# Attention scores as three rounded passes, with the next pair's projections ahead of the last mix

## The chip, the cores and the metric

The kernel runs on one core of one Trainium2 chip. The metric is the device time of one execution in microseconds (us); lower is better. Times below are of one profiled execution where a trace is read, and the median of three runs for the kernel as a whole.

## The reference

Two layers of a mixer and an MLP, on 512 latent tokens and 256 context tokens of width 1024. In each layer a projection of the normalised input is split among three mixers (latent attention, a Fourier mix, a state space), whose outputs are gated, summed and projected; then an MLP with squared ReLU. The change concerns the attention alone:

```python
qn, qr = mla_q(za, lp["q_norm"], lp["w_uq"])      # 8 heads, 64 + 32 rotary
qr = apply_rope(qr, cos[:, None, :], sin[:, None, :])
kn, v, kr = mla_kv(za, lp["kv_norm"], lp["w_ukv"]) # one rotary key for all heads
kr = apply_rope(kr, cos, sin)
...
s = jnp.einsum('bqhd,bkhd->bhqk', q_nope, k_nope) + jnp.einsum('bqhr,bkr->bhqk', q_rope, k_rope)
p = jax.nn.softmax(s * ATTN_SCALE, axis=-1)
return jnp.einsum('bhqk,bkhd->bqhd', p, v)
```

Latent queries attend to context and latent keys (768), context queries to context keys alone (256). In layer 1 only latent queries are wanted (n is 512 there, 768 in layer 0).

## The kernel before, in words

All engines run programs written out by hand, and wait for each other by semaphores; the order on each engine is the order of the code. Each large product multiplies a weight tile of 128 output channels by up to 768 tokens. To keep float32 accuracy, a product is made in three passes of rounded parts (type fp32r): high weights by high tokens, high weights by low tokens, low weights by high tokens (`product`, line 464, and `project`, line 918). The high part is a copy to fp32r, by ScalarE, the low part is a subtraction, value less high part, by VectorE. GpSimd splits the weights (lines 1284, 1287) from tiles that SyncE loads into a ring; a tile's place comes free when `w_used` is marked.

The tail of the projections (`slots`): after the gates, `("key", 0)`, `("query", 0)`, `("query", 1)` project the keys and both queries of the first pair of heads, and the last gate tile (23) follows. A slot's bank of PSUM is `TURN[s % 4]`.

Attention runs over four pairs of heads (`h2`). One pair has units (head j, block b of 128 queries): 12 in layer 0, of which the last four have 256 keys, and 8 in layer 1. For a unit u, TensorE makes the scores (line 1048, plain float32, 96 partitions, in banks 0 and 1), VectorE the row maximum (`maximum`, line 2034), ScalarE the exponent (line 1661), VectorE the reciprocal and the division (line 2050), TensorE the transposes (line 1096, bank 2), ScalarE their copy (line 1684), and TensorE the mix with the values (`mix`, line 1063, bank 3), in thirds for each group of four units. TensorE's order is scores(u + 2), perhaps a third of a mix, then the transposes of u. In layer 0 the modulation's products (`pe_ada`, line 582) lie between.

At the hand-over from one pair to the next, TensorE projects the first query of the next pair (`project_q(h2 + 1, 0)`, bank 0) among the last units, then does the modulation's turn (line 592, layer 0 only) and the last mix; then the keys (`project_k`, bank 2), the second query (bank 1), scores(0), the projection of the values (`project_v`, line 944, bank 3), scores(1). Of the queries, ScalarE copies the 64 plain rows (line 1591) and VectorE rotates the 32 rotary rows (`rotate`, lines 1824, 1826, 1829), straight from PSUM; ScalarE copies the keys (lines 1583, 1584). The output of a pair in bank 3 is rounded by ScalarE (`oah`, line 1698), and its low part is VectorE's (`oal`, line 2064, `ol_ready`); the next values may be written to the bank after that.

In pair 1 ScalarE also rounds the outputs of the state space and the Fourier mix (`osh`, `ofh`, line 1676), one a unit, and in pair 2 VectorE makes their low parts (`osl`, `ofl`, line 2057). The branches (`branch`) need these.

## Time and profile before

| | |
|---|---|
| median of three runs | 2192.99 us (2192.02 to 2195.16) |
| the profiled execution | 2193.51 us, its span 2191.7 us |
| TensorE busy | 98% of the span, 12388 products |
| VectorE, ScalarE, GpSimd busy | 56%, 23%, 41% |
| granted TensorE clock, mean | 0.996 |
| line 464 (all large products), share of the chain that ended last | 67% |
| line 1048 (scores), share of that chain | 3% |

The busy time of an engine is the union of its instructions. The chain is followed back from the last instruction, at each step to what released it; the time on it is time that the end depended on. The attention of layer 0 stands at 420 to 594 us, that of layer 1 at 1594 to 1721 us.

### The profile page before, as it was taken

The numbers are of one execution on the slowest core, as the hardware profiler recorded it, in microseconds if no ns is written. First come the engines' busy times: TensorE is split into PE (matmuls) and PEld (weight loads), VectorE is DVE, ScalarE is ACT, GpSimd is POOL, SyncE is SP. The second block draws the span as 40 slices with busy tenths as digits, with TensorE's granted clock in tenths as the row PEclk, the third lists the DMA queues.
The fourth block names the chain that finished last, engine by engine and source line by source line (L and its number), as shares of the span: only waits on it lengthen the run. The fifth ranks groups of instructions, "written<-read, shape, count | busy, mean of one in ns | idle before, by whom it ended". The sixth has DMA issues, their size and how long they took to land.

```text
span 2191.7 us, 30382 instructions
## 1 busy us (share of the span) xinstructions
PE 2147.6 (98%) x12388; PEld 1759.2 (80%) x12388; DVE 1225.6 (56%) x1887; ACT 505.0 (23%) x814; POOL 898.6 (41%) x492
## 2 busy tenths in 40 slices
PE   6999999999999999999999999999999999999998
PEld 4888888766688888888888888888766787888886
DVE  7998981455563445364565424594255757253353
ACT  3115021354400220110201102322355212010010
POOL 2441442200144344443444443545411356766662
PEclk9999999999999999999999999999999999999998
DMA  7363354233453422122223254546310552322221
GB/s 279 103 136 99 123 191 138 92 109 117 166 197 118 172 105 95 67 75 90 77 87 101 73 220 184 116 141 207 125 39 14 195 187 81 114 96 96 96 97 67
DMA packets 105390, 267.79 MB, mean 122 GB/s; under 512 B 22650, under 2 KB 42490, under 8 KB 103470
## 3 DMA queue, kind: packets, MB, share of 16 engines
q1 hardware_dynamic: 68928, 190.87, 25.4%
q10 hardware_dynamic: 36334, 75.07, 10.5%
q8 instruction: 98, 1.61, 0.3%
q14 instruction: 30, 0.25, 0.0%
HBM read 227.56 MB, written 37.88 MB: 121 GB/s over the span
## 4 chain that ended last, share of the span: by engine, by line
PE 90%; DVE 7%; DMA 1%; SPq 1%; ACT 1%; issue 0%; POOL 0%; DVEq 0%; ACTq 0%; POOLq 0%
PE ps L464 67%; PE ps L1048 3%; PE ps L918 3%; PE ps L1063 2%; PE ps L1096 2%; PE ps L582 2%; PE ps L473 2%; DVE t_out L2170 1%; DVE t_in L2170 1%; PE ps L479 1%; PE ps L956 1%; PE ps L777 1%; PE ps L991 1%; PE ps L944 1%; PE ps L907 1%; DMA ada_first<-in_ada_w 1%
## 5 line engine op out<-in xcount | busy, mean ns | idle before, releaser
L1284 POOL TENSOR_SCALAR whi<-raw 128x1024 fp32r<-128x1024 f32 x244 | 272.3, 1116 | 1240.3 <-PE ps L464 679.0
L1287 POOL TENSOR_TENSOR wlo<-raw,whi 128x1024 fp32r<-128x1024 f32 x244 | 626.8, 2569 | 20.4
L464 PE MATMUL ps<-hh,whi 128*128 128x512 f32 (+1 forms) x1560 | 465.3, 355 | 0.3 <-DVE ada L608 0.3
L464 PE MATMUL ps<-hh,wlo 128*128 128x512 f32 (+1 forms) x1560 | 462.8, 353 | 0.0
L464 PE MATMUL ps<-hl,whi 128*128 128x512 f32 (+1 forms) x1560 | 461.7, 352 | 0.0
L464 PEld LDWEIGHTS ps<-hh,whi 128*128 128x128 f32 x1560 | 254.8, 188 | 44.1 <-ACT mr L1718 1.0
L464 PEld LDWEIGHTS ps<-hl,whi 128*128 128x128 f32 x1560 | 254.3, 188 | 42.8 <-issue 0.2
L464 PEld LDWEIGHTS ps<-hh,wlo 128*128 128x128 f32 x1560 | 254.2, 188 | 42.1
L2103 DVE SCALAR_TENSOR_TENSOR x<-ps,ada,x 128x512 f32<-128x512 f32 x120 | 75.5, 659 | 343.0 <-PE ps L464 342.9
L464 PE MATMUL ps<-midh,whi 128*128 128x512 f32 (+1 forms) x768 | 233.8, 358 | 1.8 <-DVE midl L2133 1.8
L464 PE MATMUL ps<-midh,wlo 128*128 128x512 f32 (+1 forms) x768 | 231.2, 355 | 0.0
L464 PE MATMUL ps<-midl,whi 128*128 128x512 f32 (+1 forms) x768 | 230.9, 355 | 0.0
L2129 DVE TENSOR_TENSOR ms<-mr 128x768 f32<-128x768 f32 (+1 forms) x64 | 76.2, 1190 | 182.6 <-ACT mr L1718 182.5
L2133 DVE TENSOR_TENSOR midl<-ms,midh 128x768 fp32r<-128x768 f32 (+1 forms) x64 | 172.7, 2699 | 2.2
L1718 ACT ACTIVATE mr<-ps 128x768 f32<-128x768 f32 (+1 forms) x64 | 45.1, 705 | 520.2 <-PE ps L464 510.7
L464 PEld LDWEIGHTS ps<-midh,whi 128*128 128x128 f32 x768 | 126.3, 188 | 25.3 <-DVE midl L2133 3.0
L464 PEld LDWEIGHTS ps<-midl,whi 128*128 128x128 f32 x768 | 126.5, 188 | 22.0
L464 PEld LDWEIGHTS ps<-midh,wlo 128*128 128x128 f32 x768 | 125.8, 188 | 21.7
L1048 PE MATMUL ps<-kk,qq 96*128 96x512 f32 (+1 forms) x288 | 104.7, 483 | 1.2 <-ACT pr L1661 1.2
L1492 ACT ACTIVATE gt<-ps,b_gate 128x768 f32<-128x768 f32 (+1 forms) x48 | 38.2, 797 | 271.2 <-PE ps L464 259.7
L2034 DVE TENSOR_REDUCE mx<-ps 128x1 f32<-128x768 f32 (+1 forms) x80 | 68.0, 850 | 54.7 <-PE ps L1048 54.2
L1048 PEld LDWEIGHTS ps<-kk,qq 96*128 96x128 f32 x288 | 48.6, 189 | 40.4 <-issue 35.9
(251 smaller groups left out, 2833.5 us busy)
## 6 DMA issues: line engine op xcount, KB each, us to landing
raw<-in_w_main SPq DMA_DIRECT2D x244, 512.0 KB, 3.3
ada_gap<-in_ada_w SPq DMA_DIRECT2D x40, 512.0 KB, 10.0
ada_mixer<-in_ada_w SPq DMA_DIRECT2D x32, 512.0 KB, 4.0
g_d<-gt ACTq DMA_DIRECT2D x24, 384.0 KB, 2.4
gl<-g_d ACTq DMA_DIRECT2D x8, 1152.0 KB, 5.9
ada_first<-in_ada_w SPq DMA_DIRECT2D x16, 512.0 KB, 15.4
cout_d<-cz SPq DMA_DIRECT2D x12, 512.0 KB, 5.1
cout<-cout_d ACTq DMA_DIRECT2D x6, 1024.0 KB, 9.1
```

The source lines that it names most:

```text
L464: ins = pe.matmul(ps[:, p % 4, a:b], ww[:, w % W_SLOTS, kw * P:(kw + 1) * P], xx[:, kx, a:b], start=(first and i == 0 and j == 0), stop=(l ...
L473: pe.matmul(ps[:, p, a:b], ww[:, w % W_SLOTS, k * P:(k + 1) * P], hh[:, k, a:b], start=(k == 0 and ww is whi), stop=False)
L582: ins = pe.matmul(sums[32 * j:32 * j + 32], svec[:, u, :], w[:, 256 * j:256 * j + 256], start=(u == 0), stop=(u == 7))
L918: ins = pe.matmul(ps[:, p, a:b], ww, xx[:, a:b], start=(first and i == 0), stop=(last and i == 2))
L1048: ins = pe.matmul(ps[:, u % 2, a:e], qq[0:96, j, b * P:b * P + P], kk[0:96, j, a:e], start=True, stop=True)
L1284: pool.tensor_scalar(whi[:, u, :], raw[:, u % 2, :], 1.0, 0.0, ALU.mult, ALU.add).then_inc(w_split.sem, 1)
L1287: pool.tensor_tensor(wlo[:, u, :], raw[:, u % 2, :], whi[:, u, :].bitcast(F32), ALU.subtract).then_inc(w_split.sem, 1)
L1718: act.activation(mr[:, m % 2, 0:n], pair(t % mlp_pairs(l), n), ACT.Relu).then_inc(relu_ready.sem, relu_ready.mark((l, q, m)))
L2034: dve.tensor_reduce(mx[:, c:c + 1], ps[:, u % 2, (0 if b < 4 else 512):TOK], AXX, ALU.max).then_inc(max_ready.sem, max_ready.mark((l, h2, u)))
L2103: ins = dve.scalar_tensor_tensor(x[:, m, a:b], pair(p, n)[:, a:b], ada[:, l, ada_tile(row, m), s:s + 1], x[:, m, a:b], ALU.mult, ALU.add)
L2129: dve.tensor_tensor(ms[:, m % 2, 0:n], mr[:, m % 2, 0:n], mr[:, m % 2, 0:n], ALU.mult).then_inc(msq_ready.sem, msq_ready.mark((l, q, m)))
L2133: dve.tensor_tensor(midl[:, m, 0:n], ms[:, m % 2, 0:n], midh[:, m, 0:n].bitcast(F32), ALU.subtract).then_inc(midl_ready.sem, midl_ready.ma ...
```

## The change

1. Scores are made in three passes of rounded parts: high query by high key, low query by high key, high query by low key, all into the same bank. For this ScalarE rounds each query whole (96 rows, after the rotation) and the keys of each head (64 rows), and VectorE subtracts to get the low parts of both. The rotation's result goes back to PSUM. The rotary rows of the keys are split once a layer by VectorE, after the copies of y.
2. At a hand-over the second query and the keys are projected before the turn and the last mix. VectorE's queue there has both rotations, then low query 0, low keys 0, low query 1, low keys 1, all ahead of the modulation's sum and `oal`; ScalarE's has the four high parts ahead of `oah`.
3. The last gate tile goes ahead of the first pair's keys and queries. After them TensorE projects the values of pair 0 into the bank that lies free, and only then makes scores(0) and scores(1). ScalarE copies the values ahead of the first exponent.
4. The low parts of the Fourier outputs move from pair 2 to the end of pair 3; the first branch product waits for those of the state space alone, the second for these.

The diff, without signals' declarations and repeated forms:

```diff
+VALUES_PAIR = (2, 3)
...
     return (gates[:before - 1] + [("y", i) for i in range(3)] + gates[before - 1:before - 1 + between]
-            + [("glu", o) for o in range(3)] + gates[before - 1 + between:-1]
-            + [("key", 0), ("query", 0), ("query", 1), gates[-1]])
+            + [("glu", o) for o in range(3)] + gates[before - 1 + between:]
+            + [("key", 0), ("query", 0), ("query", 1)])
...
+        kkh = rest("kkh", 15360, [P, 2, TOK], F32R)
+        kkl = (rest("kkl0", 86016, [P, TOK], F32R), at("kkl1", HREG + 27648, [P, TOK], F32R))
+        qqh = rest("qqh", 49152, [P, 2, TOK], F32R)
+        qql = [at(f"qql{j}", HREG + 30720 + 3072 * j, [P, TOK], F32R) for j in range(2)]
+        qqt = [at(f"qqt{j}", HREG + 30720 + 3072 * j, [P, TOK]) for j in range(2)]
...
-                    if j:
+                    if j and h2 == 0:
...
-                ins.then_inc(k_done.sem, k_done.mark((l, h2)))
-
-            def project_v(h2):
+                if h2:
+                    ins.then_inc(w_used.sem, w_used.mark(t0 + pair_tile(h2)))
+                else:
+                    ins.then_inc(k_done.sem, k_done.mark((l, h2)))
...
+                    pe.wait_ge(os_lo.sem, os_lo.at((l, 2)))
+                elif seq == 1:
                     pe.wait_ge(os_lo.sem, os_lo.at((l, 5)))
...
-                if h2:
-                    project_k(h2)
-                    project_q(h2, 1)
-                pe.wait_ge(ropes.sem, ropes.at(("q", l, h2, 0, 2)))
-                pe.wait_ge(q_act.sem, q_act.at((l, h2, 0)))
-                pe.wait_ge(k_act.sem, k_act.at((l, h2)))
-                if h2 == 0:
-                    pe.wait_ge(ropes.sem, ropes.at(("k", l, 3)))
...
-                    if u == 1:
-                        pe.wait_ge(ropes.sem, ropes.at(("q", l, h2, 1, 2)))
-                        pe.wait_ge(q_act.sem, q_act.at((l, h2, 1)))
+                    if u < 2:
+                        pe.wait_ge(q_lo.sem, q_lo.at((l, h2, j)))
+                        pe.wait_ge(k_lo.sem, k_lo.at((l, h2, j)))
                     if u >= 2:
                         pe.wait_ge(exp_ready.sem, exp_ready.at((l, h2, u - 2)))
                     keys = spans(TOK) if b < 4 else [(512, 768)]
-                    for a, e in keys:
-                        ins = pe.matmul(ps[:, u % 2, a:e], qq[0:96, j, b * P:b * P + P], kk[0:96, j, a:e],
-                                        start=True, stop=True)
+                    qh, ql = (v[0:96, b * P:b * P + P] for v in (qqh[:, j], qql[j]))
+                    for i, (q, k) in enumerate(((qh, kkh[:, j]), (ql, kkh[:, j]), (qh, kkl[j]))):
+                        for a, e in keys:
+                            ins = pe.matmul(ps[:, u % 2, a:e], q, k[0:96, a:e], start=(i == 0), stop=(i == 2))
                     ins.then_inc(sc_done.sem, sc_done.mark((l, h2, u)))
...
-                scores(0)
-                if h2:
+                if h2 == 0:
+                    pe.wait_ge(g_ready.sem, g_ready.at((l, N_GATES - 1)))
+                    if l:
+                        pe.wait_ge(k_lo.sem, k_lo.at((l, 0, 1)))
+                    project_v(0, VALUES_PAIR[l])
+                    pe.wait_ge(kr_split.sem, kr_split.at((l, "low")))
+                    pe.wait_ge(k_lo.sem, k_lo.at((l, 0, 1)))
+                    scores(0)
+                    scores(1)
+                else:
+                    scores(0)
                     pe.wait_ge(ol_ready.sem, ol_ready.at((l, h2 - 1)))
-                elif l == 0:
-                    pe.wait_ge(ropes.sem, ropes.at(("q", 0, 0, 1, 2)))
-                    pe.wait_ge(q_act.sem, q_act.at((0, 0, 1)))
-                project_v(h2)
-                if l == 0 and h2 == 0:
-                    pe.wait_ge(g_ready.sem, g_ready.at((0, N_GATES - 1)))
-                scores(1)
+                    project_v(h2)
+                    scores(1)
...
-                        pe.wait_ge(g_ready.sem, g_ready.at((l, N_GATES - 1)))
+                        pe.wait_ge(v_act.sem, v_act.at((l, 0)))
...
                 if h2 < 3:
                     project_q(h2 + 1, 0, range(2, KQ))
+                    pe.wait_ge(exp_ready.sem, exp_ready.at((l, h2, len(units) - 1)))
+                    project_q(h2 + 1, 1)
+                    pe.wait_ge(pt_evac.sem, pt_evac.at((l, h2, len(units) - 1)))
+                    project_k(h2 + 1)
                 else:
                     branch(0)
                 if l == 0:
...
-            def copy_keys(h2, p=2):
-                act.wait_ge(k_done.sem, k_done.at((l, h2)))
-                act.copy(kk[0:64, 0, :], ps[0:64, p, 0:TOK])
-                act.copy(kk[0:64, 1, :], ps[64:128, p, 0:TOK]).then_inc(k_act.sem, k_act.mark((l, h2)))
-
-            def copy_query(h2, j, p):
-                if j:
+            def copy_keys(h2, j, p=2):
+                if h2:
                     act.wait_ge(w_used.sem, w_used.at(l * N_TILES + pair_tile(h2)))
                 else:
-                    act.wait_ge(q_done.sem, q_done.at((l, h2, 0)))
-                act.copy(qq[0:64, j, 0:n], ps[0:64, p, 0:n]).then_inc(q_act.sem, q_act.mark((l, h2, j)))
+                    act.wait_ge(k_done.sem, k_done.at((l, h2)))
+                act.copy(kkh[0:64, j, :], ps[64 * j:64 * j + 64, p, 0:TOK]).then_inc(k_hi.sem, k_hi.mark((l, h2, j)))
+
+            def copy_query(h2, j, p):
+                act.wait_ge(ropes.sem, ropes.at(("q", l, h2, j, 2)))
+                act.copy(qqh[0:96, j, 0:n], ps[0:96, p, 0:n]).then_inc(q_hi.sem, q_hi.mark((l, h2, j)))
...
-                if h2:
-                    copy_query(h2, 0, 0)
-                    copy_keys(h2)
-                    copy_query(h2, 1, 1)
...
-                exponent(0)
+                if h2:
+                    exponent(0)
                 act.wait_ge(v_done.sem, v_done.at((l, h2)))
-                act.copy(vv[:].rearrange("p b v -> p (b v)"), ps[:, 3, 0:TOK]).then_inc(v_act.sem, v_act.mark((l, h2)))
+                act.copy(vv[:].rearrange("p b v -> p (b v)"), ps[:, 3 if h2 else VALUES_PAIR[l], 0:TOK]).then_inc(
+                    v_act.sem, v_act.mark((l, h2)))
+                if h2 == 0:
+                    exponent(0)
...
+                if h2 < 3:
+                    for j in range(2):
+                        copy_query(h2 + 1, j, j)
+                        copy_keys(h2 + 1, j)
                 act.wait_ge(pv_done.sem, pv_done.at((l, h2, groups - 1)))
                 act.copy(oah[:, h2, 0:n], ps[:, 3, 0:n]).then_inc(oh_ready.sem, oh_ready.mark((l, h2)))
...
-        def rotate(dve, src, dst, part, n, key):
+        def rotate(dve, src, part, second, n, key):
 
             dve.tensor_tensor(part[64:96, 0:n], src[64:96, 0:n], rope[64:96, 0:n], ALU.mult).then_inc(
                 ropes.sem, ropes.mark((*key, 0)))
-            dve.tensor_tensor(dst[0][64:96, 0:n], src[96:128, 0:n], rope[96:128, 0:n], ALU.mult).then_inc(
+            dve.tensor_tensor(second[64:96, 0:n], src[96:128, 0:n], rope[96:128, 0:n], ALU.mult).then_inc(
                 ropes.sem, ropes.mark((*key, 1)))
             dve.wait_ge(ropes.sem, ropes.at((*key, 1)))
-            dve.tensor_tensor(dst[0][64:96, 0:n], dst[0][64:96, 0:n], part[64:96, 0:n], ALU.add).then_inc(
+            dve.tensor_tensor(part[64:96, 0:n], second[64:96, 0:n], part[64:96, 0:n], ALU.add).then_inc(
                 ropes.sem, ropes.mark((*key, 2)))
-            if len(dst) > 1:
-                dve.wait_ge(ropes.sem, ropes.at((*key, 2)))
-                dve.tensor_copy(dst[1][64:96, 0:n], dst[0][64:96, 0:n]).then_inc(ropes.sem, ropes.mark((*key, 3)))
...
-            rotate(dve, kk[:, 1], (kk[:, 0], kk[:, 1]), kk[:, 1], TOK, ("k", l))
...
+            dve.wait_ge(ropes.sem, ropes.at(("k", l, 2)))
+            dve.tensor_copy(kkh[64:96, 0, :], kk[64:96, 1, :]).then_inc(kr_split.sem, kr_split.mark((l, 0)))
+            dve.wait_ge(snat_act.sem, snat_act.at(l))
+            dve.wait_ge(kr_split.sem, kr_split.at((l, 0)))
+            dve.tensor_tensor(kkl[0][64:96, :], kk[64:96, 1, :], kkh[64:96, 0, :].bitcast(F32), ALU.subtract).then_inc(
+                kr_split.sem, kr_split.mark((l, 1)))
+            dve.wait_ge(kr_split.sem, kr_split.at((l, 1)))
+            dve.tensor_copy(kkh[64:96, 1, :], kkh[64:96, 0, :].bitcast(F32)).then_inc(
+                kr_split.sem, kr_split.mark((l, 2)))
...
+
+            def rotate_query(h2, j, p):
+                if j and h2 == 0:
+                    dve.wait_ge(w_used.sem, w_used.at(l * N_TILES + pair_tile(0)))
+                else:
+                    dve.wait_ge(q_done.sem, q_done.at((l, h2, j)))
+                rotate(dve, ps[:, p, :], ps[:, p, :], qqt[j], n, ("q", l, h2, j))
+
+            def low_query(h2, j, p):
+                dve.wait_ge(q_hi.sem, q_hi.at((l, h2, j)))
+                dve.tensor_tensor(qql[j][0:96, 0:n], ps[0:96, p, 0:n], qqh[0:96, j, 0:n].bitcast(F32),
+                                  ALU.subtract).then_inc(q_lo.sem, q_lo.mark((l, h2, j)))
+
+            def low_keys(h2, j, p=2):
+                dve.wait_ge(k_hi.sem, k_hi.at((l, h2, j)))
+                dve.tensor_tensor(kkl[j][0:64, :], ps[64 * j:64 * j + 64, p, 0:TOK], kkh[0:64, j, :].bitcast(F32),
+                                  ALU.subtract).then_inc(k_lo.sem, k_lo.mark((l, h2, j)))
+
+            pairs = [TURN[order.index(("query", j)) % 4] for j in range(2)]
+            for j in range(2):
+                low_keys(0, j, TURN[order.index(("key", 0)) % 4])
+            dve.tensor_copy(kkl[1][64:96, :], kkl[0][64:96, :].bitcast(F32)).then_inc(
+                kr_split.sem, kr_split.mark((l, "low")))
+            for j in range(2):
+                rotate_query(0, j, pairs[j])
+            for j in range(2):
+                low_query(0, j, pairs[j])
             for h2 in range(4):
-                for j in range(2):
-                    if j:
-                        dve.wait_ge(w_used.sem, w_used.at(l * N_TILES + pair_tile(h2)))
-                    else:
-                        dve.wait_ge(q_done.sem, q_done.at((l, h2, 0)))
-                    if j or h2:
-                        dve.wait_ge(ropes.sem, ropes.at(("q", l, h2 - (1 - j), 1 - j, 2)))
-                    p = j if h2 else TURN[order.index(("query", j)) % 4]
-                    rotate(dve, ps[:, p, :], (qq[:, j],), ps[:, p, :], n, ("q", l, h2, j))
                 units = [(j, b) for b in range(nq) for j in range(2)]
 
                 def maximum(u):
@@ -2051,11 +2093,21 @@
                                                        None, ALU.mult).then_inc(p_ready.sem, p_ready.mark((l, h2, u)))
                     if u + 2 < len(units):
                         maximum(u + 2)
-                    if h2 == 2 and u < 6:
-                        hi, lo, src = ((osh, osl, osm), (ofh, ofl, of))[u // 3]
+                    if h2 == 2 and u < 3:
                         dve.wait_ge(os_hi.sem, os_hi.at((l, u)))
-                        dve.tensor_tensor(lo[:, u % 3, 0:n], src[:, u % 3, 0:n], hi[:, u % 3, 0:n].bitcast(F32),
+                        dve.tensor_tensor(osl[:, u, 0:n], osm[:, u, 0:n], osh[:, u, 0:n].bitcast(F32),
                                           ALU.subtract).then_inc(os_lo.sem, os_lo.mark((l, u)))
+                if h2 < 3:
+                    for j in range(2):
+                        rotate_query(h2 + 1, j, j)
+                    for j in range(2):
+                        low_query(h2 + 1, j, j)
+                        low_keys(h2 + 1, j)
+                else:
+                    for i in range(3):
+                        dve.wait_ge(os_hi.sem, os_hi.at((l, 3 + i)))
+                        dve.tensor_tensor(ofl[:, i, 0:n], of[:, i, 0:n], ofh[:, i, 0:n].bitcast(F32),
+                                          ALU.subtract).then_inc(os_lo.sem, os_lo.mark((l, 3 + i)))
...
-        main += [gates[:-1], heads[0][None], gates[-1:], np.stack(heads[1:])]
+        main += [gates, np.stack(heads)]
```

## Rows read from the trace of the kernel before

**Rows 1.** The page, busy time of each engine (share of span) and count.

```profile
PE 2147.6 (98%) x12388; PEld 1759.2 (80%) x12388; DVE 1225.6 (56%) x1887; ACT 505.0 (23%) x814; POOL 898.6 (41%) x492
```

**Rows 2.** The page's costliest groups: busy and mean ns, then idle before.

```profile
L1048 PE MATMUL ps<-kk,qq 96*128 96x512 f32 (+1 forms) x288 | 104.7, 483 | 1.2 <-ACT pr L1661 1.2
```

**Rows 3.** Chain of waits, hand-over to pair 1, layer 0: start, us, what.

```profile
456.75 1.05 PE ps L918 x6
...
459.16 5.50 PE ps L918 x30
464.65 1.29 PE ps L1048 x4
465.95 2.68 PE ps L944 x24
468.63 1.31 PE ps L1048 x4
...
471.88 0.88 PE ps L1096 x6
```

**Rows 4.** Timeline, VectorE and ScalarE, layer 0: start, us, engine, line, operation.

```profile
409.16 0.97 DVE L1824 TENSOR_TENSOR ps<-ps,rope 32x768 f32<-32x768 f32 x1 [14.97 <-PE ps L918]
...
460.03 0.17 DVE L608 TENSOR_TENSOR ada<-ps,early 128x16 f32<-128x16 f32 x1 [7.81 <-ACT oah L1698]
...
460.24 0.96 DVE L2064 TENSOR_TENSOR oal<-ps,oah 128x768 fp32r<-128x768 f32 x1
...
464.69 0.79 ACT L1591 COPY qq<-ps 64x768 f32<-64x768 f32 x1 [1.58 <-PE ps L918]
```

**Rows 5.** Timeline, unit loop of pair 0, layer 0.

```profile
430.13 0.87 PE L1096 MATMUL ps<-early,pr 128*128 128x128 f32 x6
430.15 0.96 DVE L2034 TENSOR_REDUCE mx<-ps 128x1 f32<-128x768 f32 x1
...
431.40 0.62 DVE L2050 TENSOR_SCALAR pr<-pr,rsm 128x768 f32<-128x768 f32 x1
...
434.25 0.88 PE L1096 MATMUL ps<-early,pr 128*128 128x128 f32 x6
```

**Rows 6.** Chain of waits, pair 0 of layer 0: gate 23, and 256-key scores.

```profile
412.17 8.33 PE ps L464 x48
...
444.84 0.43 PE ps L1048 x2
```

**Rows 7.** Timeline, then chain, hand-over to pair 1, layer 1.

```profile
1589.02 0.70 DVE L1824 TENSOR_TENSOR ps<-ps,rope 32x512 f32<-32x512 f32 x1
...
1618.49 0.48 PE L918 MATMUL ps<-zqh,whi 128*128 128x512 f32 x1
...
1619.63 2.81 PE ps L1063 x24
1622.44 4.37 PE ps L918 x21
...
1634.03 0.88 PE ps L1096 x6
```

**Rows 8.** Chain of waits, pair 2 of layer 1.

```profile
1674.93 0.60 DVE ofl L2057
```

**Rows 9.** Timeline, end of gate 23 and table loads, layer 0.

```profile
376.98 1.28 ACT L1622 ACT_TABLE_LOAD   x1 [0.44 <-ACT gt L1492]
379.51 0.90 ACT L1622 ACTIVATE yp<-ps,b_glu 128x768 f32<-128x768 f32 x1 [1.24 <-PE ps L991]
...
424.26 1.28 ACT L1661 ACT_TABLE_LOAD   x1 [2.83 <-DMA g_d<-gt]
...
428.00 0.82 PE L1096 MATMUL ps<-early,pr 128*128 128x128 f32 x6
```

**Rows 10.** Timeline of TensorE, then the busy row with the granted clock.

```profile
34.43 0.59 PE L473 MATMUL ps<-hh,whi 128*128 128x512 f32 x2 [2.96 <-ACT hh L1342]
...
36.00:39.00 3.00, 3.00 (x22) 1.76 (x24) 2.96 (x5) 1.12 (x2) 1.71 (x2) 0.50 0.46 175
```

## What the change does to the time

> **What bounds the kernel now.** I read the page first: TensorE is busy 98% of the span [rows 1], so time moves only if TensorE gets less work or stands idle longer. Then the costliest groups, for the line that the change rewrites: the scores, 288 records at line 1048 [rows 2]. A float32 product leaves two records, so these are 144 products for 64 units of 768 keys and 16 units of 256. Then the chain of waits over the hand-over from one pair of heads to the next [rows 3]: from the last tile of the next query (ends 457.80) to the first transposes (471.88) every piece is TensorE back to back, except the last 1.95 us after the second scores. VectorE had slack there, because its rotations ran under the projections. Last, timelines of VectorE and ScalarE, for what each operation costs [rows 4, 5].
>
> I write a hand-over in microseconds after t, the end of the next first query's projection.
>
> **Part 1, three passes instead of float32.** A 768-key unit costs 1.29 us now [rows 3]. Three passes of rounded parts over 768 columns are what one tile of a projection is: 1.05 us for six records [rows 3]. Saved 0.25. A 256-key unit costs 0.43 [rows 6]. A tile of 512 plus 256 columns takes 0.35 a pass; 512 alone takes 0.23 (4.37 for q1 and keys, less a start of 0.2 and the keys' six passes, 2.1, over q1's 9 [rows 7]); 256 take 0.12, three passes 0.35: saved 0.08. If all of it reached the end: 64 x 0.25 + 16 x 0.08 = 17.3 us. That is not what arrives:
>
> - The first three scores of each pair of heads lie in the hand-over, which part 2 counts whole (24 units; unit 2's scores hide under VectorE's 1.95 us). 40 units stay.
> - Units 3 to 5 of layer 0, and 3 to 6 of layer 1, run in a loop that isn't TensorE alone: scores, row maximum, exponent, division, transposes. Two units took 4.12 us [rows 5] against 2 x (0.7 + 1.29) = 4.0 of TensorE work. From a unit's scores to the next transposes lie the start of the maximum (0.2), 0.96, some 0.3 of small operations, 0.62 and a start, some 2.1; the loop over two units holds transposes (0.7), one score product and this 2.1. One score is in it, not two, so 0.25 saved is 0.12 a unit. VectorE's own load (1.87 a unit, from the maximum's start to the division's end [rows 5]) stands right behind. I take 0.12; bounds 0 and 0.25.
> - Where the modulation's products or the mix follow, TensorE bounds: units 6 and 7 of layer 0, 7 of layer 1, at 0.25, and four of 256 keys at 0.08.
> - Pair 1: ScalarE's extra rounding copies already make its loop as long; the 0.12 units give nothing. Pair 2: VectorE's low parts are on the path. Three of the six leave it; in layer 0 it is TensorE's turn by then, in layer 1 the fourth was still on the path (0.60 [rows 8]) and is gained.
>
> Layer 0: pairs 0 and 3, 3 x 0.12 + 2 x 0.25 + 4 x 0.08 = 1.2 each; pairs 1 and 2, 0.84 each; 4.1. Layer 1: pairs 0 and 3, 4 x 0.12 + 0.25 = 0.73; pair 1, 0.25; pair 2, 0.6 + 0.25; 2.6. Part 1 gives **-6.7**, bounds -11.5 (40 units whole) and -5.
>
> **Part 2, the hand-over of layer 0 (three times).** TensorE's work is only reordered: q1 and keys (5.50) go ahead of the last mix, turn and mix follow, so it is done at t + 6.86 (459.16 - 457.80 + 5.50) [rows 3]. What is new is VectorE's row. One rotation is three operations of 0.97 and their gaps, 3.0 us [rows 4]. A low part is a subtraction from PSUM of 96 or 64 partitions by 768; not in this trace, but the low part of the output, 128 x 768 from PSUM, is: 0.96 [rows 4], 1.0 with the gap to the next. All of it is queued ahead of the output's low part, for which the projection of the values waits:
>
> - rotation of query 0: t + 0.25 to 3.2; of query 1 (its projection ends at 3.13): 3.4 to 6.3. ScalarE's high parts (0.79 each [rows 4]) fit beside: query 0 by 4.1, keys 0 by 6.3, query 1 by 7.2, keys 1 by 8.0, the output's by 8.8.
> - low query 0 to 7.4, low keys 0 to 8.4. Only then scores(0): 8.4 to 9.5. TensorE has stood idle 1.6.
> - low query 1 to 9.4, low keys 1 to 10.4, modulation 0.2, output's low part to 11.6. Then the values 11.65 to 14.3: idle 2.2 more.
> - scores(1) to 15.4, and the same 1.95 to the transposes: 17.3.
>
> Before: 471.88 - 457.80 = 14.1 [rows 3]. So **+3.2 each, +9.9 for three** (one carries a small operation on the gains more, some 0.2). The bound upward is another 0.4 a low part if 96 partitions at once cost more (+5 for all); downward, if such a subtraction took what the division of a row takes (0.62 [rows 5]) it would be 4 x 0.35 less, -4.2 for three.
>
> **Part 3, the hand-over of layer 1 (three times).** 512 columns: a rotation is 3 x 0.70 plus gaps, 2.2 [rows 7]. TensorE has q1 and keys 4.37 and all three thirds of the mix 2.81 [rows 7], until t + 7.2. VectorE: rotations to 4.7, low query 0 to 5.4, low keys 0 to 6.4 (before TensorE is free), low query 1, low keys 1 to 8.1, output's low part to 8.9. scores(0) 7.2 to 8.25, values 8.9 to 11.6, scores(1) 12.6, transposes 14.6. Before, from the same t (1618.49 plus 0.7) to 1634.03: 14.85 [rows 7]. **-0.5 for three**; bounds -2 and +2.
>
> **Part 4, the start, once a layer.** Before, gate 23 (8.3 us) lay over the rotations, and from its end (420.50 [rows 6]) to the first transposes it took 7.5: scores, values, scores, then ScalarE held by the gate's store and 1.28 of table load [rows 9]. Now gate 23 is ahead, and from the end of query 1 at T: rotation 0 ends T + 0.1 (VectorE still has two low keys and a copy before it), rotation 1 T + 3.2, low query 0 T + 4.2; the values, done at T + 2.7, cover only part. scores(0) to 5.3, low query 1 to 5.2, scores(1) to 6.4, maximum 5.5 to 6.5, exponent 6.7 to 7.6, scores(2) to 8.7, transposes 8.7. The gate's store has long landed, and the table load hides: that at 376.98 was done at 378.26, while its activation waited for TensorE until 379.51 [rows 9]. Layer 0: +1.2. Layer 1: rotation 0 ends T + 1.7, 1 T + 3.9, transposes T + 9.05 against 7.4 of before: +1.6. **+2.8**; if the table load came after the wait it would be 1.28 more each, +5.4; if the rows of VectorE ran 0.3 shorter each, +1.
>
> The Trainium skill (ScalarE: Activation LUTs, Rules for kernel authors) budgets some 2.7 us for a change of table set, and the trace has 1.28 [rows 9]; by the page's figure the load would end after the maximum and the start would cost some 1.3 us more a layer, 2.6 in all. The row decides.
>
> **The rest at nothing.** The rotary key's split (two copies and a subtraction of 32 partitions) stands on VectorE between the copies of y and the arrival of y by DMA. VectorE waits for that DMA far longer than three such operations take (a pass over 768 elements is 0.97 [rows 4]); if the cover failed it would be 3 us once a layer. The three Fourier low parts of the last pair (0.96 each at most, as in [rows 4]) run under the first branch product (nine passes, 3.1), turn and mix; without cover they would cost 2.9. Tile order in the weights changes nothing on SyncE's or GpSimd's queue: the same tiles in nearly the same order, and the modulation's loads start earlier. The waits for the last exponent and the last copy of transposes sit behind matmuls longer than both.
>
> **Sum.** -6.7 + 9.9 - 0.5 + 2.8 = +5.5 us. On the profiled execution's 2193.5 (span 2191.7 and 1.8 around it) that is 2199.0; the median is 0.5 lower, so **2198.5**.
>
> **Rivals.**
>
> - *The gain is whole* (0.20): the unit loop is bound by TensorE after all, since transposes show stalls and refills that a shorter score absorbs. For it: 4.12 is more than TensorE's 4.0. Against: ends of the maximum coincide with starts of the transposes. Then -11.5 + 9.9 - 0.5 + 2.8 = +0.7: 2193.7, no change.
> - *VectorE's row is shorter* (0.12), the side of faster. Place: the hand-overs of layer 0. If low parts and rotations overlap so that the output's low part is ready at t + 9 and not 11.6, TensorE waits for it 0.1 us at most, each hand-over costs 0.6, and the sum is -6.7 + 1.8 - 1 + 1 = -5: 2188. It decides from the point where the row of eight operations ends before t + 9.8. Against: every 768-column operation from PSUM in the timeline takes 0.95 to 0.97 and starts after its predecessor [rows 4].
> - *The clock falls* (0.13). TensorE stood idle for 2.96 us before 34.43, and from 36 to 39 the granted clock was 0.50, the lower level of 1.2 GHz [rows 10]. In layer 0's hand-overs it now idles 1.6 and 2.2 us around one score product. If that has the same effect, 3 us of matmuls at half the pace cost 1.5 each, 4.5 to 5 in all: 2203. Against: the waits that already stand in the attention left no mark in the page's clock row. The Trainium skill (TensorE: Matmul & The Clock Gate, HAM oscillation) says that matmul bursts with waits between them come out at the half clock again and again; here that would hit only the three hand-overs.
> - *The passes are not cheaper* (0.05): if 96-row products of rounded parts fell to float32's pace per pass, a unit would cost 1.29 or more and part 1 be nothing or negative: 2205 to 2212. Against: all projections run at 0.35.
>
> The forecast itself has 0.50. Its own range is 2195 to 2202. With the rivals' ends 2190 to 2206 holds eight in ten: it leaves out most of the fast rival and the last. What a measurement here can tell from no change is about 0.2%, 4.4 us. Faster by more than that: the fast rival, 0.12. Within: the whole gain, and the part of the forecast below 2197.4, 0.20 + 0.11 = 0.31. Slower: 0.57.
>
> **What the profile after would show.** Scores in records of two spans by three passes, about 1.05 us a unit. In layer 0 each hand-over: TensorE idle about 1.6 us before scores(0), released by VectorE's low keys, and about 2.2 before the values, released by the output's low part; about 17.3 from t to the transposes. Layer 1: one idle of 0.6 before the values. The unit loop at 1.95 a unit instead of 2.06. Granted clock 1.00 throughout. I am wrong if low parts take clearly less or more than 0.96, if the loop's pitch falls by 0.2 or more, or if TensorE's idle stretches stand elsewhere.

## The result and the profile after

The changed kernel took 2208.76 us (median of 6 runs, 2206.46 to 2211.26); the kernel before, beside it, 2194.28 (6 runs, 2192.02 to 2198.57). The ratio is 1.0063, 95% interval 1.0053 to 1.0073: 14 us slower, 10 more than the 2198.5 that I gave and above the range's end of 2206. A later measurement (e11_after, below) gave 2206.41 against 2193.82, ratio 1.0046 (1.0029 to 1.0064). The profiled execution took 2206.46 with a span of 2204.7, which is 13.0 above the span before; the accounts below are made against that.

The page of the changed kernel: busy time of each engine with its share and count, then the chain that ended last by engine. Against [rows 1] TensorE has 5.5 us *less* busy time, so what it stood idle grew by 18.5 us.

```profile
PE 2142.1 (97%) x12532; PEld 1781.9 (81%) x12532; DVE 1262.3 (57%) x1925; ACT 506.3 (23%) x814; POOL 901.7 (41%) x492
...
PE 87%; DVE 10%; DMA 1%; ACT 1%; issue 1%; SPq 0%; POOL 0%; DVEq 0%; POOLq 0%; ACTq 0%
```

The chain of waits through the hand-over to pair 1 of layer 0, the stretch that [rows 3] show of before (start, us, what). The end of the first query's projection, t, is 459.6 (462.76 less the 3.13 us of the second query's). The expectations that I wrote for the experiments take it 0.2 earlier: their t + 11.2 and t + 18.9 are t + 11.0 and t + 18.7 here.

```profile
458.58 4.18 PE ps L926 x24
...
462.79 0.97 DVE ps L1842
463.76 0.03 issue
463.79 0.97 DVE qqt L1844
464.76 0.02 issue
464.79 0.97 DVE ps L1847
...
465.78 0.95 DVE qql L2052
466.74 0.73 DVE kkl L2057
...
467.52 0.94 DVE qql L2052
468.46 0.03 issue
468.49 0.96 DVE kkl L2057
...
469.49 0.19 DVE ada L616
469.69 0.97 DVE oal L2116
470.66 0.04 issue
470.71 4.57 PE ps L955 x24
475.28 1.07 PE ps L1055 x6
```

Before, the whole chain here was TensorE; now VectorE's row carries it for 7.9 us, from the second rotation (L1842 to L1847) through four low parts (L2052, L2057) to the output's (L2116). That is what was forecast, and nearly when: output's low part done at t + 11.0, forecast 11.6. What was not forecast is the line behind it. The values' projection (L955, 24 records) took 4.57 us, where [rows 3] have 2.68 for the same 24 records. Part of the difference is the wait itself: behind an idle stretch and at full clock they take 2.92 (e10_second_idle, below). The other 1.65 us are the clock's.

TensorE's timeline of the same place shows the two idle stretches, in brackets with what ended them. The busy row by windows (columns: length; busy time of TensorE, its weight load, VectorE, ScalarE, GpSimd, each with its count; granted clock; DMA share; GB/s) shows why the values are slow.

```profile
467.75 0.59 PE L1055 MATMUL ps<-kkh,qqh 96*128 96x512 f32 x2 [1.56 <-DVE kkl L2057]
...
470.71 4.57 PE L955 MATMUL ps<-vw,zkv 128*128 128x128 f32 x24 [1.67 <-DVE oal L2116]
...
478.30 0.87 PE L1106 MATMUL ps<-early,pr 128*128 128x128 f32 x6 [0.93 <-DVE pr L2092]
```

```profile
468.00:470.00 2.00, 1.04 (x6) 0.62 (x5) 1.90 (x4) 0.23 (x1) 0.53 (x1) 1.00 0.00 0
470.00:472.00 2.00, 1.29 (x7) 1.29 (x8) 1.67 (x3) 0.26 (x1) 0.00 (x0) 0.78 0.00 0
472.00:474.00 2.00, 2.00 (x12) 2.00 (x11) 0.00 (x0) 0.73 (x2) 0.00 (x0) 0.50 0.00 0
474.00:476.00 2.00, 2.00 (x14) 1.90 (x14) 0.00 (x0) 0.68 (x1) 0.00 (x0) 0.87 0.00 0
```

The granted clock is 1.00 until TensorE has been idle twice, then 0.50 (the lower level, 1.2 GHz), then 1.00 again (the windows of 0.78 and 0.87 hold some of both). In the page's 40 slices nothing of this is to be seen; a slice is 55 us long. The second and third hand-overs of layer 0, and the start of layer 1, in the chain:

```profile
518.59 4.57 PE ps L955 x24
...
568.15 5.49 PE ps L955 x24
...
1611.02 3.90 PE ps L1055 x12
```

The last line is two units' scores, three passes each; behind the same wait at full clock they take 2.3 us (e4_oal). In the timeline they follow 1.99 us of idle time, and in windows of 2 us the granted clock was 0.79, then 0.50. At the third hand-over it was down from the values' first product on:

```profile
567.00:569.00 2.00, 0.85 (x4) 0.85 (x5) 1.93 (x4) 0.00 (x0) 0.00 (x0) 0.50 0.00 0
569.00:571.00 2.00, 2.00 (x11) 2.00 (x11) 0.15 (x1) 0.99 (x2) 0.00 (x0) 0.50 0.00 0
571.00:573.00 2.00, 2.00 (x11) 2.00 (x10) 0.00 (x0) 0.00 (x0) 0.00 (x0) 0.50 0.00 0
```

Layer 1's hand-overs have hardly any idle time (0.18 us ahead of the values), and keep their clock:

```profile
1642.78 2.94 PE ps L955 x24
```

Where the 13.0 us of the spans lie, measured between the same marks in both traces (first work of each attention, which is the scores before and the values after; first and last transposes of each pair; first branch product):

| stretch | forecast | measured |
|---|---|---|
| ahead of the attention of layer 0 | 0 | +1.25 |
| start of layer 0 (7.67 to 9.12) | +1.2 | +1.45 |
| three hand-overs of layer 0 (15.5, 15.5, 15.6 to 20.1, 20.1, 21.2) | +9.9 | +14.8 |
| unit loops of layer 0 (0.9, 0.8, 0.8, 1.0) | -4.1 | -3.4 |
| between the attentions of the two layers | 0 | -1.9 |
| start of layer 1 (7.39 to 10.69) | +1.6 | +3.3 |
| rest of layer 1's attention | -3.1 | -2.6 |
| sum | +5.5 | +12.9 |

The first line is the low clock near the start of the program that [rows 10] show, which lasted a little longer in this execution (mean granted clock from 30 to 40 us: 0.71 against 0.83); it has no place in the change. A hand-over is counted here from the last transposes of one pair to the first of the next. The -1.9 I have not traced to a line: each trace has one 100 us window at 0.98 in the stretch, and nothing else stands out. The change does not touch this stretch (587.6 to 1594.0 before, 1006.4 us, 1004.5 after), and the other traces have 1002.9 to 1008.8 for it, so -1.9 is within what it varies.

### The profile page after: what moved, and what is told of

Same layout as the page of the kernel before. It is cut to its first block, busy times and chain, and to the rows that moved or that the text cites. A ratio compares the mean times of both kernels' runs of the same rounds, so it can differ in the third digit from the quotient of the medians.

```text
span 2204.7 us, 30697 instructions
## 1 busy us (share of the span) xinstructions
PE 2142.1 (97%) x12532; PEld 1781.9 (81%) x12532; DVE 1262.3 (57%) x1925; ACT 506.3 (23%) x814; POOL 901.7 (41%) x492
## 4 chain that ended last, share of the span: by engine, by line
PE 87%; DVE 10%; DMA 1%; ACT 1%; issue 1%; SPq 0%; POOL 0%; DVEq 0%; POOLq 0%; ACTq 0%
PE ps L472 66%; PE ps L1055 2%; PE ps L1106 2%; PE ps L481 2%; PE ps L926 2%; PE ps L590 2%; PE ps L1069 2%; DVE t_out L2222 2%; DVE t_in L2222 1%; PE ps L955 1%; PE ps L487 1%; PE ps L785 1%; PE ps L967 1%; PE ps L1002 1%; DVE mx L2076 1%; PE ps L915 1%
## 5 line engine op out<-in xcount | busy, mean ns | idle before, releaser
L2181 DVE TENSOR_TENSOR ms<-mr 128x768 f32<-128x768 f32 (+1 forms) x64 | 81.9, 1280 | 181.2 <-ACT mr L1736 180.9
L2185 DVE TENSOR_TENSOR midl<-ms,midh 128x768 fp32r<-128x768 f32 (+1 forms) x64 | 167.8, 2622 | 2.4 <-DVE ms L2181 0.3
L1322 ACT ACTIVATE sqt<-x 128x768 f32<-128x768 f32 (+1 forms) x40 | 30.1, 759 | 199.5 <-DVE x L2155 179.4
L1698 ACT COPY pt<-ps 128x768 f32<-128x768 f32 (+1 forms) x80 | 57.4, 717 | 66.2 <-PE ps L1106 65.3
```

What stands on the lines that cost most here:

```text
L1698: act.copy(pts[pt_slot(l, h2, g)][:, j, k0:6, q0:q0 + P], ps[:, 2, k0 * P:TOK].rearrange("p (k q) -> p k q", q=P)).then_inc(pt_evac.sem, p ...
L2181: dve.tensor_tensor(ms[:, m % 2, 0:n], mr[:, m % 2, 0:n], mr[:, m % 2, 0:n], ALU.mult).then_inc(msq_ready.sem, msq_ready.mark((l, q, m)))
L2185: dve.tensor_tensor(midl[:, m, 0:n], ms[:, m % 2, 0:n], midh[:, m, 0:n].bitcast(F32), ALU.subtract).then_inc(midl_ready.sem, midl_ready.ma ...
```

## The experiments

All ratios are to the kernel before, run beside them on the same chip (2192.71 us in the first set, 2193.56 in the second, 2193.82 in the third).

**Filling the idle time (e1_fill).** If the clock falls because TensorE stands idle, products that nobody reads must hold it up. The edit puts them between the waits:

```diff
                     if u < 2:
                         pe.wait_ge(q_lo.sem, q_lo.at((l, h2, j)))
+                        if l == 0 and h2 and u == 0:
+                            warm(0, 2)
                         pe.wait_ge(k_lo.sem, k_lo.at((l, h2, j)))
...
+                    if l == 0 and h2 and u == 0:
+                        for _ in range(4):
+                            for a, e in keys:
+                                pe.matmul(ps[:, 0, a:e], qh, kkh[0:96, j, a:e], start=True, stop=True)
```

`warm(p, count)` is `count` float32 products of 256 columns into buffer p; at the starts of the two layers 3 and 4 of them follow the values.

> The changed kernel, its order kept, with products that nobody reads placed where TensorE stood idle: in layer 0's hand-overs two float32 products of 256 columns between the waits for low query 0 and low keys 0, and four more high-by-high passes at the head of scores(0) (overwritten by the real ones); at the starts three (layer 0) and four (layer 1) such products after the values' projection. They fit into the idle time. Theory 1, the clock: the values' 24 products took 4.57, 4.57 and 5.49 us in layer 0 and the first two scores of layer 1 took 3.90 because the granted clock fell to 0.50 after the idle stretches. With TensorE kept busy it stays at 1.00, the values take 2.7, the three hand-overs go from 18.9, 18.9 and 20.0 to 17.0 to 17.3, the start of layer 1 gains 1.8: 7 to 9 us less than the changed kernel, about 2200. Theory 2, the values are slowed by something beside the clock's fall (VectorE and ScalarE at PSUM, the weights): nothing changes, 2206 to 2210.

Measured: 2198.0 us (12 runs), ratio 1.0027 (1.0017 to 1.0037). Timeline of TensorE in the first hand-over, and the window on the values:

```profile
466.14 1.13 PE L1045 MATMUL ps<-rope,early 128*128 128x256 f32 x4 [0.61 <-DVE qql L2064]
467.00 1.67 PE L1063 MATMUL ps<-kkh,qqh 96*128 96x512 f32 x8
...
470.05 2.95 PE L955 MATMUL ps<-vw,zkv 128*128 128x128 f32 x24 [0.34 <-DVE oal L2128]
```

```profile
470.00:472.00 2.00, 1.95 (x17) 1.95 (x18) 1.01 (x2) 0.92 (x2) 0.00 (x0) 1.00 0.00 0
```

TensorE was given more work, the values took 2.95 in all three hand-overs, the clock stayed at 1.00 and the kernel was 8 us faster by the ratios. The values still started at t + 11: VectorE's row had not moved. So the excess over the forecast is the clock, and at these places it is the idle time that brings it. The three hand-overs took 18.5, 18.5 and 18.7 us instead of 20.1, 20.1 and 21.2: 5.8 us for the clock. **e8_fillho** leaves the two starts unfilled (the same edit without their `warm`).

> The changed kernel with filling products at layer 0's hand-overs alone, none at the two starts. Against the kernel that fills both (2198.0) the starts' share is what they took there and without: layer 0's start 8.94 against 9.12 us, layer 1's 9.36 against 10.69, so 1.5 us more, about 2199.5. If the clock at the hand-overs is not the main cause, it is near 2205.

Measured: 2200.86 (5 runs), 1.0035 (1.0022 to 1.0047), values 2.94 three times; the first two scores of layer 1 ran slow again, 3.9 us. By the traces the hand-overs are thus most of the clock's price and the starts the smaller part: layer 1's start took 10.7 us, against 9.6 for the same code at full clock (e4_oal), so 1.1.

**The order alone (e3_f32).** The changed order, with plain float32 scores on the high parts and no low parts of queries and keys. The block shows the scores; the subtractions of both are left out as well:

```diff
-                    for i, (q, k) in enumerate(((qh, kkh[:, j]), (ql, kkh[:, j]), (qh, kkl[j]))):
-                        for a, e in keys:
-                            ins = pe.matmul(ps[:, u % 2, a:e], q, k[0:96, a:e], start=(i == 0), stop=(i == 2))
+                    for a, e in keys:
+                        ins = pe.matmul(ps[:, u % 2, a:e], qh.bitcast(F32), kkh[0:96, j, a:e].bitcast(F32),
+                                        start=True, stop=True)
...
```

> The changed kernel's order on every engine, with scores in plain float32 as before, and without the low parts (they are not needed). Against the kernel before this is the reordering alone. By my account of e2 about 8 us above e2: 6.7 for the unit loops and some 2 for scores in hand-overs and starts, so 2202 to 2204, 8 to 10 above the kernel before. If the reordering were free, 2194.

Measured: 2202.24 (5 runs), 1.0050 (1.0037 to 1.0063). The time is the expected one, its basis is not: it was to be 8 us above e2_nolow, and e2_nolow, which follows, came out only 3 below it (5 by the ratios). VectorE's low parts are gone, yet the values still wait, since ScalarE's copies stand ahead of the output's high part: 1.81, 1.80 and 2.01 us of idle time, and 4.57, 4.57 and 2.94 us for the values. The third kept its clock after the longest of the three.

**No low parts, three passes (e2_nolow).** Each pass takes high part by high part, and VectorE has nothing to subtract for queries and keys. The block shows the scores:

```diff
-                    for i, (q, k) in enumerate(((qh, kkh[:, j]), (ql, kkh[:, j]), (qh, kkl[j]))):
+                    for i, (q, k) in enumerate(((qh, kkh[:, j]), (qh, kkh[:, j]), (qh, kkh[:, j]))):
...
```

> The changed kernel without the low parts of queries and keys on VectorE (sixteen operations on queries, sixteen on keys); all three passes take high by high, so TensorE's work is the same. It leaves out the correction by the low parts. Theory 1, VectorE's row makes the idle time: the output's low part is ready at t + 9.8 (ScalarE's rounding then ends last) and not 11.2, scores(0) go at t + 6.9; hand-overs of layer 0 fall from 18.9 to 20.0 down to 15.5, each start by 1, layer 1's start by its clock too: 12 to 15 us less than the changed kernel, about 2195. Theory 2, the reordering itself (projections ahead of the mix, values between) costs what was lost: at most 4 us less.

Measured: 2199.39 (10 runs), 1.0026 (1.0017 to 1.0035). It missed the 2195: the output's low part was ready at t + 9.8, as expected, but the part of the gain that was to come from the clock did not.

```profile
468.78 4.58 PE L955 MATMUL ps<-vw,zkv 128*128 128x128 f32 x24 [2.04 <-DVE oal L2114]
...
515.56 4.17 PE L955 MATMUL ps<-vw,zkv 128*128 128x128 f32 x24 [2.04 <-DVE oal L2114]
...
563.97 4.57 PE L955 MATMUL ps<-vw,zkv 128*128 128x128 f32 x24 [2.25 <-DVE oal L2114]
```

Taking four subtractions off VectorE moves the limit to ScalarE's row of high parts, at whose end the output's stands. One idle stretch of 2.0 to 2.3 us was enough for the clock to fall, three times of three. In this profile, of the slowest of the ten runs, it fell at both starts too: in layer 0 behind 1.63 us of idle time ahead of the third scores, which then took 1.85 us, in layer 1 behind 1.47.

**The passes alone (e6_passes).** The order before, one unsplit rounded query and key, three passes over them. The block shows the scores; the copies ahead of them change their type:

```diff
-                    for a, e in keys:
-                        ins = pe.matmul(ps[:, u % 2, a:e], qq[0:96, j, b * P:b * P + P], kk[0:96, j, a:e],
-                                        start=True, stop=True)
+                    for i in range(3):
+                        for a, e in keys:
+                            ins = pe.matmul(ps[:, u % 2, a:e], qq[0:96, j, b * P:b * P + P], kkr[0:96, j, a:e],
+                                            start=(i == 0), stop=(i == 2))
...
```

> The kernel before, its order kept, with three rounded passes in place of each float32 score, all three of the rounded query by the rounded keys, so no low parts are made. It leaves out the correction by the low parts; it is the gain of part 1 alone. The forecast's loop account: 6.7 in the unit loops and 0.5 in each of six hand-overs, 10 us less than the kernel before, 2184. The rival that the gain is whole: 17 less, 2177.

Measured: 2184.32 (5 runs), 0.9956 (0.9943 to 0.9968). That is near the forecast's account (half of a score's saving arrives in the loops) and far from the rival's in which all of it does. In the trace, 9.1 us shorter than before, the unit loops gained 4.4 us, not 6.7, the six hand-overs 2.9 and the two starts 0.7. It is also what the passes would be worth if high and low parts cost nothing.

**VectorE's row reordered (e4_oal).** All the products of the change, but the output's low part now stands third behind the rotations instead of fifth:

```diff
                 if h2 < 3:
                     for j in range(2):
                         rotate_query(h2 + 1, j, j)
-                    for j in range(2):
-                        low_query(h2 + 1, j, j)
-                        low_keys(h2 + 1, j)
+                    low_query(h2 + 1, 0, 0)
+                    low_keys(h2 + 1, 0)
...
                 dve.tensor_tensor(oal[:, h2, 0:n], ps[:, 3, 0:n], oah[:, h2, 0:n].bitcast(F32),
                                                     ALU.subtract).then_inc(ol_ready.sem, ol_ready.mark((l, h2)))
+                if h2 < 3:
+                    low_query(h2 + 1, 1, 1)
+                    low_keys(h2 + 1, 1)
```

On ScalarE the second keys' high part likewise goes behind the output's.

> The changed kernel with the output's low part moved ahead of the second query's and keys' low parts on VectorE (and the output's high part ahead of the second keys' high part on ScalarE). By the theory of two causes (VectorE's row of low parts holds up the values' projection, and the idle time this makes lets the clock fall), the values start about 1.5 us earlier (t+9.2 in place of t+11.2 and after a shorter idle stretch of about 1.3 us in all), they take 2.8 us at full clock in place of 4.6, and the first transposes stand at about t+15.0 in place of t+18.9: 3 times -3.9, so about 2196 to 2197 against 2208.8 for the change. Rival, one idle stretch of any length lets the clock fall: the values still take 4.6 us, 2202 to 2203. Rival, the row of VectorE is not what the values wait for: no gain, 2208.

Measured: 2197.02 (11 runs), 1.0014 (1.0005 to 1.0023), the time that the theory of two causes expected. The profiled execution is the fastest of the eleven, 2190.07. From the start of the last transposes of a pair to the first of the next it took 16.54 us, against 20.10 in the changed kernel and 15.51 before. One idle stretch is left, and the values follow the scores at once:

```profile
464.68 0.59 PE L1055 MATMUL ps<-kkh,qqh 96*128 96x512 f32 x2 [1.56 <-DVE kkl L2059]
...
465.82 2.84 PE L955 MATMUL ps<-vw,zkv 128*128 128x128 f32 x24
```

At layer 1's start this execution had the same idle stretch as the changed kernel (2.03 us; there 1.99, and 2.03 in e11_after) and kept its clock: the two scores behind it took 2.3 us, not 3.9. So the stretch makes a fall possible and does not settle it.

**Reordered and filled.** **e5_oal_fill** adds `warm(0, 2)` ahead of the first scores in layer 0's hand-overs and 3 and 4 products at the starts; **e12_oal_starts** adds those at the starts alone.

> The kernel before it (output's low part ahead) with the products that fill TensorE's idle time at the hand-overs of layer 0 and at both starts of the attention. If the clock already holds at the hand-overs, only the starts gain: 1 to 2 us under that kernel, about 2195. If the clock falls there, this one takes it back: 6 us and more under that kernel. If both run alike, the starts' clock is worth nothing.

> The changed kernel with the output's low part ahead and filling products at the two starts alone. With both fillings it took 2192.4, with none 2197.0. If only the starts' clock still varies from one execution to the next (the hand-overs have one idle stretch of 1.56 us and hold their clock), this equals 2192.4 or lies a little under it, since the filling at the hand-overs moved their first scores back by 0.3 to 1 us. If the hand-overs fall in part of the executions too, it is 2195 or more.

Measured: 2192.41 (12 runs), 0.9997 (0.9987 to 1.0007) with both; 2196.47 (12 runs), 1.0013 (1.0004 to 1.0022) with the starts alone. The hand-overs of all three profiled executions kept their clock (values 2.84 to 2.94), and still filling them is worth 4 us in the median. That is the case which the expectation gave for falls in part of the executions. No profile shows such a fall, so it is argued and not shown. For it: the profiles of e4_oal and e12_oal_starts are of the fastest of 11 runs and the second of 12, and the runs of e4_oal go from 2190.07 at a mean granted clock of 0.996 to 2198.82 at 0.992. Against leaning on that: the kernel before, beside it, goes from 2189.89 at 0.994 to 2198.51 at 0.993. Products that nobody reads thus make the change as fast as the kernel before. No kernel with all of the computation was faster than before.

**Idle time without the change.** Three kernels put idle time into the kernel before and nothing of the change. **e7_idle** computes the output's low part three times in layer 0's hand-overs, which pushes the first query's rotation back. **e10_second_idle** lets the values wait for the second query's rotation. **e9_two_idles** does both. The first block is e7_idle's, the second e10_second_idle's:

```diff
+                if l == 0 and h2 < 3:
+                    for i in range(2):
+                        dve.tensor_tensor(oal[:, h2, 0:n], ps[:, 3, 0:n], oah[:, h2, 0:n].bitcast(F32),
+                                          ALU.subtract).then_inc(extra.sem, extra.mark((h2, i)))
+                        dve.wait_ge(extra.sem, extra.at((h2, i)))
...
+                if l == 0 and h2:
+                    pe.wait_ge(ropes.sem, ropes.at(("q", l, h2, 1, 2)))
                 project_v(h2)
```

> The kernel before the change, with the output's low part computed three times in place of once at the three hand-overs of layer 0. It pushes the first query's rotation back by 2.0 us and so makes one idle stretch of 1.8 to 2.0 us ahead of the next pair's first scores, in place of none; the values follow the scores at once. If one such stretch alone leaves the clock up: values 2.8 us, +2.0 at each of three places, about 2198.6. If it lets the clock fall as in the changed kernel: scores and values take 1 to 2 us more each time, 2202 to 2205.

> The kernel before the change with the second of these idle stretches alone (1.6 us between first scores and values; the output's low part is computed once, so nothing is idle ahead of the scores). By the theory one stretch leaves the clock up: values 2.84 us, the kernel 3 times 1.6 us slower at most, 2195 to 2198. Rival, it is this place or this stretch that does it: values 4.6 us and 2202 or more.

> The kernel before the change with two idle stretches of TensorE at each of layer 0's three hand-overs: the one of 1.6 us ahead of the first scores (made by the repeated output's low part, where the values then still took 2.84 us) and a second of about 1.6 us between these scores and the values, which here wait for the second query's rotation. By the theory (it is the second idle stretch, so soon behind the first, that lets the clock fall) the values take 4.6 us, though nothing of the change is in the kernel, and the hand-over is 3.5 us longer than with one stretch: about 10 us more in all. Rival, the fall belongs to something else of the change (the three passes, the work on VectorE beside it): the values take 2.84 us and only the wait itself adds, 1.6 us each, 5 us.

Measured: e7_idle 2202.32 (7 runs, 2196.70 to 2206.90), 1.0039 (1.0024 to 1.0053). Its median is in the range expected for a fall, 2202 to 2205, but its profiled execution (2199.21, span 5.7 above before) kept its clock, with values of 2.84 us. Whether others fell at the hand-overs is not shown. e10_second_idle 2200.21 (8 runs), 1.0034 (1.0022 to 1.0046), between the 2195 to 2198 of the theory and the 2202 of its rival. e9_two_idles 2210.98 (6 runs), 1.0079 (1.0064 to 1.0094), span 16.3 above. In the profile of e9_two_idles the clock fell at the third hand-over and not at the first two:

```profile
467.70 1.56 PE L1049 MATMUL ps<-kk,qq 96*128 96x512 f32 x4 [1.56 <-DVE qq L1832]
470.80 2.92 PE L945 MATMUL ps<-vw,zkv 128*128 128x128 f32 x24 [1.54 <-issue]
...
564.73 1.56 PE L1049 MATMUL ps<-kk,qq 96*128 96x512 f32 x4 [1.77 <-DVE qq L1832]
567.83 5.46 PE L945 MATMUL ps<-vw,zkv 128*128 128x128 f32 x24 [1.54 <-issue]
```

In e10_second_idle it was the second, after a single stretch:

```profile
467.26 2.92 PE L944 MATMUL ps<-vw,zkv 128*128 128x128 f32 x24 [1.79 <-issue]
...
513.37 4.50 PE L944 MATMUL ps<-vw,zkv 128*128 128x128 f32 x24 [1.79 <-issue]
```

So the fall needs nothing of the change; idle time in the kernel before is enough. But my theory that the second of two stretches always does it is refuted, and so is the one that a single stretch never does. The expectation for e9_two_idles (+10) came out by its time, not by its mechanism: against e7_idle's its first two hand-overs were only 1.8 us longer, the wait itself, and the third 4.6.

Every one of the fourteen traces also has a wait that the change does not touch, 1.83 us between two large products in the middle of the program. Before, the clock held behind it; in the changed kernel it fell (the first wait's row and window, then the second's):

```profile
1111.22 0.62 PE L464 MATMUL ps<-midh,whi 128*128 128x512 f32 x2 [1.83 <-DVE midl L2133]
1112.00:1114.00 2.00, 2.00 (x39) 1.50 (x38) 1.43 (x3) 0.36 (x1) 1.18 (x2) 1.00 0.00 0
...
1121.48 0.62 PE L472 MATMUL ps<-midh,whi 128*128 128x512 f32 x2 [1.83 <-DVE midl L2185]
1123.00:1125.00 2.00, 2.00 (x34) 1.43 (x23) 1.97 (x4) 0.36 (x1) 1.92 (x2) 0.51 0.03 8
```

It fell there in six of the fourteen (the changed kernel, e1_fill, e8_fillho, e12_oal_starts, e10_second_idle, e9_two_idles). This is one and the same wait, and some executions fall behind it and others not.

**The changed kernel again (e11_after).**

> The changed kernel once more, for its time and clock beside the others on the same chip: 2206 to 2211, with 4.6 us for the values at the hand-overs of layer 0.

Measured: 2206.41 (6 runs), 1.0046 (1.0029 to 1.0064); values 4.57, 4.55 and 5.33; the start of layer 1 slow again. Two of the six took 2198.76 and 2199.33, some 7 us less than the others; the profiled one is the slowest, 2207.67. All profiled hand-overs of layer 0 together:

| kernel | idle before scores, us | idle before values, us | values, us |
|---|---|---|---|
| changed | 1.56 | 1.67 to 1.88 | 4.57, 4.57, 5.49 |
| changed, again | 1.55 | 1.69 to 1.88 | 4.57, 4.55, 5.33 |
| e2_nolow | 0 | 2.04 to 2.25 | 4.58, 4.17, 4.57 |
| e3_f32 | 0 | 1.80 to 2.01 | 4.57, 4.57, 2.94 |
| e9_two_idles | 1.56 to 1.77 | 1.54 | 2.92, 2.92, 5.46 |
| e10_second_idle | 0 | 1.73 to 1.79 | 2.92, 4.50, 2.92 |
| e7_idle, e4_oal, e12_oal_starts | 1.55 to 1.77 | 0 | 2.84 to 2.94, nine times |
| e1_fill, e8_fillho, e5_oal_fill | 0.60 to 0.61 | 0 to 0.56 | 2.85 to 2.95, nine times |

## Why the prediction was wrong

*The step that failed* is "Granted clock 1.00 throughout". It rested on the sentence against the third rival, that waits already in the attention leave no mark in the page's clock row. That was weak evidence twice over. The row's slices are 55 us, in which two or three us at half clock hardly show, and the trace of before had no idle stretch of this length in layer 0's hand-overs to be marked by. The one row that was of the right kind, [rows 10], said that a stretch of 2.96 us was followed by 0.50, and I gave it 0.13. I overlooked two waits of that trace outside the attention, 1.83 us at 1109.39 and 1.78 at 1822.68. The clock held behind both. Behind the first that was luck: it fell there in six traces of fourteen. In the sum the clock's term was nothing; the runs showed 6.9 us in its place.

*The rival that came true was itself undersized.* It said 1.5 us at each of three places, 2203. The values took 1.65, 1.65 and 2.6 more than the 2.92 that they need behind a wait at full clock, 5.9 in all, and e1_fill gives 5.8 back. The rival also looked only at the hand-overs. By the forecast's own numbers layer 1's start had idle time from T + 2.7 to the scores. Its two scores took 3.90 in place of 2.3, of which 1.1 reached the transposes (10.7 us against e4_oal's 9.6). Together 6.9 us; with the forecast's 5.5 that is 12.4, and the spans differ by 13.0. The smaller misses nearly cancel: 1.25 at the program's start, -1.9 between the layers, some 1 us less in the hand-overs, and 0.2 to 0.7 more at each of the starts, in layer 0's loops and in the rest of layer 1.

*Part 1, the loops, was right in kind and too large in size.* Layer 0 gained 3.4 of 4.1 us and layer 1 1.8 of 2.6, 5.2 of 6.7, inside the bound of 5; e6_passes by itself has 4.4. The pitch of two shared units was as forecast: 4.12 before, 3.90 after (transposes at 432.83 and 436.73), 1.95 a unit. So about half of a score's saving arrives in a loop that VectorE and TensorE share. The rival of the whole gain fell there.

*Part 2, VectorE's row, was right in place, order and nearly in size.* The low parts took 0.94 to 0.96 from PSUM whether 64 or 96 partitions wide, so neither bound was reached. Idle stretches of 1.56 and 1.67 to 1.88 stood where 1.6 and 2.2 were forecast. Without the clock the three hand-overs come to 14.8 - 5.9 = 8.9 against 9.9. The fast rival, a row that ends before t + 9.8, fell: it ended at t + 11.0, and e4_oal, where the output's low part is done at t + 9.0, shows what such an end is worth.

*Part 3 and the rest at nothing* held. Layer 1's hand-overs gained 0.27 us each, 0.8 for three, against 0.5; the forecast's own 14.6 against 14.85 makes 0.75. TensorE waited 0.18 us ahead of the values there, where 0.6 was forecast. Two of layer 0's three Fourier low parts took 1.8 and 3.1 us where 0.96 was the most, but no product waited for them.

*Part 4* was right for layer 0 (+1.45 against +1.2; the table load hid, at 426.31, ahead of an exponent at 428.50), and short for layer 1 even without the clock (3.3 - 1.1 = 2.2 against 1.6).

The Trainium skill (TensorE: Matmul & The Clock Gate, HAM oscillation) says that bursts of products with waits between them fall back to the half clock repeatedly. The waits of its example, for DMA, are some 3 to 5 us, longer than any in the attention here. I had cited it beside the rival and held that it would hit only the hand-overs. In the two profiles of the changed kernel the trace agrees, behind waits of 1.6 to 2.0 us, in eight places of the ten in the attention that have them: all six hand-overs of layer 0 and both starts of layer 1, but neither start of layer 0, where 1.6 us of idle time left the clock at 1.00.

What stays open is what settles a fall. With a stretch of 1.5 to 2.3 us ahead of the values it came in 13 of 18 profiled hand-overs; with the stretch ahead of the scores alone in none of nine; with stretches up to 0.6 in none of nine. The first none of nine is weaker than it looks, since its three profiles are of the fastest, the second and the third fastest run of their kernels. Longer idle time goes loosely with more falls, but e9_two_idles has about the changed kernel's two stretches and fell once in three, and the wait of 1.83 us in mid-program fell six times in fourteen. Idle time is not the only way down either: in the trace of before the clock is 0.50 from 746 to 748, where TensorE was busy throughout; ahead of it stand 12 records of products of 2 columns (742.04) and 12 more (744.37). What else decides was not tested.

## What to carry to other kernels

When a change adds idle time to the engine that bounds a kernel, price the stretch and then the work behind it: that work can run at half the clock, and the page's slices are too long to show it, so look at windows of 2 us. Put what a bound engine waits for first in the row of its producer. Here a change of order on VectorE and ScalarE alone was worth 7 to 11 us (ratio 1.0014 against 1.0046 and 1.0063), about what the three passes gain by themselves (0.9956). An engine that is busy with nothing of use can be faster than one that waits.

## What the runs showed of the hardware that I had not expected

- The granted clock fell from 1.00 to 0.50 after idle stretches much shorter than the 2.96 us of [rows 10]: once after a single 1.79, and in the changed kernel after 1.56 and 1.67 with 1.1 us of products between them. It did so in some executions of the same code and not in others: layer 1's start after 1.99 and 2.03 us of idle time fell in three profiles (twice the changed kernel, e8_fillho) and held in one (e4_oal), and 1.83 us in mid-program fell in six of fourteen.
- In e1_fill 2.3 us of products that nobody reads made the first hand-over 1.6 us shorter (last transposes of a pair to the first of the next, 18.47 against 20.10), since the clock stayed up.
- Runs of one kernel spread over 9 us with or without the change (e4_oal 2190.07 to 2198.82 in 11 runs; the kernel before, beside it, 2189.89 to 2198.51 in 24), so one profiled execution stands for its kernel only where its time is near the median.
